# Differential attention's norms at other units, an 8 KB factor spread, split tables and a re-ordered first and last stretch in a two-layer decoder trunk

## The reference, cut to what matters

```python
for l in range(2):
    h = rmsnorm(x, norm_mix[l])
    u, sq, sk, sv, dq, dk, dv, gate_logits = split(h @ w_in[l])
    y_ssm = gelu(s5_ssm(u, lam_re, lam_im, log_dt, b, c, d))   # 32 groups, 64 complex states each
    glu_a, glu_b = split(y_ssm @ w_glu[l]);  y_ssm = glu_a * sigmoid(glu_b)
    y_sb = stick_breaking_attention(sq, sk, sv)                # 8 heads of 64
    o = differential_attention(rope(dq), rope(dk), dv, lam)    # 4 heads, v of 128
    o = rmsnorm(o, diff_subln[l]) * (1 - lam_init)             # over each head's 128
    proj = einsum('bsnc,ncd->bsnd', [y_ssm, y_sb, o], w_branch[l])
    x = x + sum(sigmoid(gate_logits) * proj) @ w_out[l]
    x = x + cross_attention(rmsnorm(x, norm_cross[l]), rmsnorm(mem, norm_mem[l]))
    x = x + square(relu(rmsnorm(x, norm_mlp[l]) @ w_up[l])) @ w_down[l]
return rmsnorm(x, norm_final)
```

## Time and profile before

| | us |
|---|---|
| median of 3 runs | 1058.99 |
| lowest, highest run | 1057.1, 1062.11 |
| the profiled execution, its own time | 1057.28 |
| its span, first to last instruction | 1055.6 |
| TensorE busy in the span | 998.8 |
| VectorE busy | 765.9 |
| ScalarE busy | 557.3 |
| GpSimd busy | 45.8 |
| mean granted TensorE clock | 0.984 of full speed |

### The profile page before, as it was taken

How to read it: one execution, slowest core, us unless ns; L and a number is a source line. 1 busy time by engine, 2 the same in 40 slices (tenths; PEclk the granted TensorE clock), 3 DMA queues, 4 the chain that set the end, 5 groups by cost and what they waited for, 6 DMA issues and landing times. The chain is left out here.

```text
span 1055.6 us, 17635 instructions
## 1 busy us (share of the span) xinstructions
PE 998.8 (95%) x6784; PEld 884.1 (84%) x6784; DVE 765.9 (73%) x1186; ACT 557.3 (53%) x847; POOL 45.8 (4%) x100
## 2 busy tenths in 40 slices
PE   6989999979999999989999999998799999999996
PEld 6867899879897888878889779998798978888885
DVE  6979897758865866869865669786687658655664
ACT  7455435476655655535453663544647556444443
POOL 5003000000000004000000110000000000000000
PEclk9999999989999999999999999999899999999998
DMA  9894348435654665596646853564365445666661
GB/s 358 208 200 145 121 130 251 140 102 180 186 154 136 224 187 178 193 204 192 188 138 201 173 159 105 138 198 145 104 183 172 142 138 180 186 193 186 191 187 74
DMA packets 71827, 181.37 MB, mean 172 GB/s; under 512 B 27392, under 2 KB 29696, under 8 KB 71360
## 3 DMA queue, kind: packets, MB, share of 16 engines
q1 hardware_dynamic: 71600, 180.23, 58.2%
q10 hardware_dynamic: 144, 0.00, 0.0%
HBM read 176.67 MB, written 3.54 MB: 171 GB/s over the span
## 5 line engine op out<-in xcount | busy, mean ns | idle before, releaser
L1262 DVE TENSOR_TENSOR s_w_lo<-s_raw,s_w_hi 128x1024 fp32r<-128x1024 f32 x312 | 374.3, 1227 | 93.6 <-ACT s_w_hi L905 90.4
L905 ACT ACTIVATE s_w_hi<-s_raw 128x1024 fp32r<-128x1024 f32 x312 | 321.1, 1054 | 189.4 <-PE p_T L1845 76.3
L1843 PE MATMUL p_T<-s_hT,s_w_hi 128*128 128x256 f32 x576 | 165.8, 288 | 0.1
L1844 PE MATMUL p_T<-s_hT,s_w_hi 128*128 128x256 f32 x576 | 162.9, 283 | 0.0
L1845 PE MATMUL p_T<-s_hT,s_w_lo 128*128 128x256 f32 x576 | 162.8, 283 | 0.0
L1843 PE MATMUL p_A<-s_w_hi,s_bT_hi 128*128 128x512 f32 x320 | 125.3, 391 | 5.3 <-DVE s_w_lo L1262 2.8
L1845 PE MATMUL p_A<-s_w_hi,s_bT_lo 128*128 128x512 f32 x320 | 124.7, 390 | 0.0
L1844 PE MATMUL p_A<-s_w_lo,s_bT_hi 128*128 128x512 f32 x320 | 124.6, 390 | 0.0
L1843 PEld LDWEIGHTS p_T<-s_hT,s_w_hi 128*128 128x128 f32 x576 | 110.3, 191 | 4.0 <-issue 2.7
L1844 PEld LDWEIGHTS p_T<-s_hT,s_w_hi 128*128 128x128 f32 x576 | 110.4, 192 | 0.1
L1845 PEld LDWEIGHTS p_T<-s_hT,s_w_lo 128*128 128x128 f32 x576 | 110.3, 192 | 0.0
(11 more groups left out here) (265 smaller groups left out, 1872.9 us busy)
## 6 DMA issues: line engine op xcount, KB each, us to landing
s_raw<-in_weights SPq DMA_DIRECT2D x312, 512.0 KB, 3.6
s_bt<-in_ssm_bt SPq DMA_DIRECT2D x2, 1024.0 KB, 11.9
s_gates<-f_turn SPq DMA_DIRECT2D x16, 128.0 KB, 8.8
s_x<-in_x SPq DMA_DIRECT2D x1, 1024.0 KB, 9.2
s_dv<-in_ssm_bc SPq DMA_DIRECT2D x2, 512.0 KB, 8.0
u_turn<-s_st_y SPq DMA_DIRECT2D x4, 256.0 KB, 5.2
s_uB<-u_turn SPq DMA_DIRECT2D x16, 64.0 KB, 4.8
s_bt<-in_mem SPq DMA_DIRECT2D x1, 1024.0 KB, 6.9
```

The lines of the kernel that those rows point to most:

```text
L905: return nc.scalar.activation(o, i, f, **kw)
L1262: return V.tensor_tensor(o, i0, i1, op)
L1843: mm(o, lhi, rhi, start=first, stop=False, **kw)
L1844: mm(o, lhi, rlo, start=False, stop=False, **kw)
```

## The change

It has six parts.

1. `da_n` of the first tile goes from unit 24 to 22; `da_o` 0, `da_c` 1 and `da_n` 1 go from unit 26 to 25. `da_o` 1 stays at 27.
2. The table of factors is stored by four transfers of 256 byte runs instead of two of 512 byte runs, in an order that lets each of the eight spreading loads read 8 KB in one run for each of its 16 partitions.
3. Layer 0's phase tables: steps 0 and 1 at unit 0 (a new stage `p_ph0`, which runs in the `stage` part), 2 and 3 at unit 6, 4 at 7, the products of step 5 at 8 and its sums at 9. Steps 0 to 3 use part of `gates` as scratch. `p_bt` 0, 1, 2 go from units 9, 10, 11 to 10, 11, 12.
4. `e16` is made on GpSimd at the start.
5. Start: ScalarE issues `x_t` part 0, `col` and `positions`; SyncE goes from chunk 0 on to `x_t` part 1. ScalarE rounds chunk 0 before it waits for `col`. VectorE's `rope_angles` (nine small operations) comes behind its work on `x_t`. `bt` is loaded behind chunk 12.
6. End: x times the last gain is done in two halves of 512 columns, the first ahead of the last unit's residual; ScalarE makes the bias after the first half's squares and takes Ln of each tile as its square is there; VectorE makes one factor `RC` and scales columns 0 to 639, ScalarE scales 640 to 1023; a store waits for both.

```diff
+END = 640
-        for k in range(TAB_STEPS):
-            after(u["ph"][max(0, k - 3)], "p_ph", tgt, k)
+        for at, k, part in u["ph"]:
+            after(at, "p_ph", tgt, k, part)
-        pre(0, dict(ct=-1, f=(2, 3), cv=(3, 4), b0=5, ph=(7, 7, 8), bt=(9, 10, 11)))
+        pre(0, dict(ct=-1, f=(2, 3), cv=(3, 4), b0=5, 
+                    ph=((6, 2, 2), (6, 3, 2), (7, 4, 2), (8, 5, 0), (9, 5, 1)), bt=(10, 11, 12)))
+        after(0, "p_ph0")
...
-    after(24, "da_n", 0)
-    after(26, "da_o", 0)
-    after(26, "da_c", 1)
-    after(26, "da_n", 1)
+    after(22, "da_n", 0)
+    after(25, "da_o", 0)
+    after(25, "da_c", 1)
+    after(25, "da_n", 1)
     after(27, "da_o", 1)
...
-                    dst = f_turn[t].rearrange("(n r i) s -> r n i s", r=2, n=BL)
                     for r in range(2):
-                        load(dst[r], fT[PC * r:PC * r + PC, :], f_out)
+                        for h in range(2):
+                            load(f_turn[t, :, h, STILES * r:STILES * r + STILES, :], fT[PC * r:PC * r + PC, PC * h:PC * h + PC],
+                                 f_out)
...
-                            load(bF[p:p + GC].rearrange("p r (i s) -> p (r i) s", s=STATES),
-                                 src[h, j].unsqueeze(0).broadcast_to([GC, 2 * STILES, STATES]), f_in)
+                            load(gates[p:p + GC, 0:8, :].rearrange("p k n -> p (k n)"),
+                                 f_turn[t, j, h].rearrange("k s -> (k s)").partition_broadcast(GC), f_in)
...
                     if l == 0 and c == 0:
-                        load_params(0)
-                        load_x_t(0)
                         load_x_t(1)
...
-                    if l == 0 and c == 6:
+                    if l == 0 and c == 12:
                         load_b(0)
...
+            act.dma_start(x_t[:, X_PARTS[0], :], a["x_t"][:, X_PARTS[0], :]).then_inc(xt_landed[0].sem, 16)
+            act.dma_start(col[:, :], a["col"][0]).then_inc(prm_landed.sem, 16)
             act.dma_start(stat[:, 62:64].bitcast(I32), a["positions"]).then_inc(pos_landed, 16)
...
-                    if which == "mix":
+                    if which == "mix" and l:
                         act.wait_ge(*st.at(prm_landed, l + 1))
...
                     if which == "mix" and l == 0:
-                        rope_angles()
                         for i, part in enumerate(X_PARTS):
...
+                        rope_angles()
                         return
...
-                        for q in range(4):
-                            n = 2 * GC * q
-                            tt(e16[n:n + 2 * GC, :], ident[n:n + 2 * GC, n:n + GC], ident[n:n + 2 * GC, n + GC:n + 2 * GC],
-                               ALU.add).then_inc(*st.mid())
-                        dve.wait_ge(*st.mine())
+                        dve.wait_ge(consts_made, 20)
...
-                def p_ph(t, k):
+                def p_ph(t, k, part=2):
...
+                    scratch = st_y[:, :, :].rearrange("p r n -> p (r n)")
+                    if t == 0 and k < 4:
+                        scratch = gates[:, 12, :]
+                    elif t == 0:
+                        dve.wait_ge(*st.at(u_out, 2))
+                    q = scratch[:, 0:2 * STILES * n].rearrange("p (r i n) -> p r i n", r=2, n=n)
+                    if part != 1:
+                        tt(o, e, c[0]).then_inc(*st.mid())
+                        tt(q, e, c[1]).then_inc(*st.mid())
+                        dve.wait_ge(*st.mine())
+                    if part:
+                        tt(o[:, 0], o[:, 0], q[:, 1], ALU.subtract).then_inc(*st.mid())
...
+                    elif kind == "p_ph0":
+                        for k in range(2):
+                            p_ph(0, k)
+                            dve.wait_ge(*st.mine())
...
+                    if l + 1 == DEPTH and u + 1 == NU:
+                        dve.wait_ge(nf_landed, 16)
+                        dve.wait_ge(*st.mine())
+                        gained(0)
...
+            gained(1)
             dve.wait_ge(end_act, 8)
...
+            V.tensor_tensor(RC, R0, TT, ALU.mult).then_inc(*est.mid())
+            dve.wait_ge(*est.mine())
             for t in range(NT):
-                V.tensor_scalar(xn[:, t, :], xn[:, t, :], R0[:, t:t + 1], TT[:, t:t + 1], ALU.mult, ALU.mult)\
-                 .then_inc(*est.mid())
+                V.tensor_scalar(xn[:, t, 0:END], xn[:, t, 0:END], RC[:, t:t + 1], None, ALU.mult).then_inc(*est.mid())
```

More of the change, by code:

```diff
@@ L513, in hybrid_trunk @@
         bt_landed = counted("bt_landed", DEPTH, step=16)
-        f_out, f_in = counted("f_out", 2 * DEPTH, step=16), counted("f_in", 2 * BL * DEPTH, step=16)
+        f_out, f_in = counted("f_out", 4 * DEPTH, step=16), counted("f_in", 2 * BL * DEPTH, step=16)
         k_out, k_in = signal("k_out", 4, step=16), signal("k_in", 2 * BL, step=16)
@@ L768, in _ @@
             for t in range(NT):
-                sp.wait_ge(end_dve, 7 + t)
+                sp.wait_ge(end_dve, 10 + t)
+                sp.wait_ge(end_scaled, 1 + t)
                 sp.dma_start(out[0].rearrange("(t p) d -> p t d", p=P)[:, t, :], xn[:, t, :]).then_inc(stored, 16)
@@ L804, in tt @@
                 return nc.gpsimd.tensor_tensor(o, i0, i1, op)
+            for q in range(4):
+                n = 2 * GC * q
+                tt(e16[n:n + 2 * GC, :], ident[n:n + 2 * GC, n:n + GC], ident[n:n + 2 * GC, n + GC:n + 2 * GC], ALU.add)\
+                    .then_inc(*cst.mid())
+            pool.wait_ge(*cst.mine())
             def tables(st, t):
@@ L956, in norm @@
                                 prep_chunk(i // 2)
+                            act.wait_ge(*st.at(prm_landed, 1))
                             act.wait_ge(*st.at(xt_landed[i], 1))
@@ L1202, in _ @@
                     if half:
-                        act.wait_ge(end_act, 1 + t)
+                        act.wait_ge(end_act, 3)
                     c = slice(512 * half, 512 * half + 512)
@@ L1206, in _ @@
                         .then_inc(end_act, 1)
-            act.wait_ge(end_act, 4)
-            fn(SS0V, SS, ACT.Identity, scale=1.0 / D, bias=eps[:, 0:1]).then_inc(end_act, 1)
-            act.wait_ge(end_act, 5)
-            for t in range(NT):
-                fn(R0[:, t:t + 1], SS1[:, t:t + 1], ACT.Ln, scale=1.0 / D, bias=SS0V[:, t:t + 1]).then_inc(end_act, 1)
+                    if half:
+                        act.wait_ge(end_act, 4 + 2 * t)
+                        fn(R0[:, t:t + 1], SS1[:, t:t + 1], ACT.Ln, scale=1.0 / D, bias=SS0V[:, t:t + 1]).then_inc(end_act, 1)
+                if half == 0:
+                    act.wait_ge(end_act, 2)
+                    fn(SS0V, SS, ACT.Identity, scale=1.0 / D, bias=eps[:, 0:1]).then_inc(end_act, 1)
             act.wait_ge(end_act, 7)
             fn(R0, R0, ACT.Exp, scale=-0.5).then_inc(end_act, 1)
+            act.wait_ge(end_dve, 9)
+            for t in range(NT):
+                fn(xn[:, t, END:], xn[:, t, END:], ACT.Identity, scale=RC[:, t:t + 1]).then_inc(end_scaled, 1)
         @block.vector
@@ L1255, in _, with gained @@
             dve.wait_ge(*pst.mine())
+            est = Steps(end_dve)
+            def gained(half):
+                c = slice(512 * half, 512 * half + 512)
+                for t in range(NT):
+                    V.tensor_tensor(xn[:, t, c], x[:, t, c], uB_flat[:, c], ALU.mult).then_inc(*est.mid())
             for l in range(DEPTH):
@@ L1799, in _ @@
                 dve.wait_ge(*st.mine())
-            est = Steps(end_dve)
-            dve.wait_ge(nf_landed, 16)
-            for t in range(NT):
-                V.tensor_tensor(xn[:, t, :], x[:, t, :], uB[:, :, :].rearrange("p i n -> p (i n)"), ALU.mult)\
-                 .then_inc(*est.mid())
+            gained(1)
             dve.wait_ge(end_act, 8)
```

23 lines of the change are left out of this document (8 added, 15 removed).

## The result

The changed kernel takes 1027.67 us, the median of four runs (1026.68 to 1028.59); the kernel before took 1058.72 us in the four runs now at hand (1057.1 to 1062.11). The ratio is 0.9702, with a 95% interval of 0.9676 to 0.9729: 31 us faster. The forecast was 1029.0 us, from a sum of 29.95 us. The profiled execution after took 1026.68 us, with a span of 1025.0 us; against the 1057.28 and 1055.6 us before, that is 30.6 us by either.

The account below looks back on a forecast made before the run. TensorE, busy nearly throughout, bounds the kernel; gains come only from its waits, low clock and ends. Norms 22.2, spread 2.75, tables 4.4 less 0.3, start -0.3, end 1.2 sum to 29.95 us: 1059.0 to 1029.0 us, range 1024 to 1034.

Parts of the forecast that it names:

- e16: Work moved from VectorE to GpSimd at the start: takes 0.76 us off VectorE's lateness, costs nothing on GpSimd, idle until 11.5.
- 214.5: Norms: the time in us when VectorE ends the second norm, before TensorE is through unit 27 at about 218.
- the drain of a table load: Norms: counting the skill's 2.66 us for load and drain would make the gain about 0.8 us less a layer.
- the limit of 12: Second spread: a transfer of anything up to 12 us was held early enough for TensorE; some 5 us were taken.
- the bound of 3: Second spread, first layer's MLP: upper bound in us of the gain, forecast at 2.75 with lower bound 0.
- the wait and its low clock: Layer 0, ahead of `sb_u` 1: 2.75 us of wait and 1.65 us of low clock go, a gain of 4.4.
- the bound, not 0.3: Start and tables up to `mm_k`: a loss of 0.3 us, bounded by a gain of 1 and a loss of 1.5.
- A: Rival: half of the second norm's wait stays, with its low clock, 12.6 us worse, 1041.6 us; chance 0.12.
- B: Rival: the tables don't pay, the mask is late again, 4.4 us gone and 1 more lost, 1034.4 us; chance 0.12.
- C: Rival: the new waits (0.85 and 0.6 twice) don't appear and the start gains 1 us, 1024.8 us; chance 0.10.
- D: Rival: the second spread still delays its chunk, 2.75 us worse, 1031.8 us; counted within the forecast's 0.63.
- E: Rival: one transfer engine carries each spreading load, eight take 43 us and stop TensorE, 1075 us; chance 0.02.

Follow-up runs that it names:

- third group: The group of runs in which the unaltered changed kernel was run again, 1027.42 us, beside the kernel before, 1055.9 us.
- norms_back: Changed kernel with `da_n` 0 back at unit 24 and `da_o` 0, `da_c` 1, `da_n` 1 back at unit 26: 1048.8 us.
- spread_back: Changed kernel with the factors stored and spread as before (two stores of 512 byte runs, eight loads of 256 byte runs): 1031.4 us.
- phases_at_6: Changed kernel with steps 0 and 1 of layer 0's phase table at unit 6 beside steps 2 and 3, none at unit 0: 1025.75 us.
- tables_back: Changed kernel with layer 0's tables as before (steps 0 to 4 at unit 7) and `e16` on VectorE again: 1030.12 us.

## Why the forecast was right, and where its steps were not

The parts, undone one by one, give 21.4 (norms), 4.0 (spread), 2.7 (tables), -0.9 (start) and 0.4 (end), 27.6 us together, by the medians. By the ratios, which take each group's own runs of the kernel before, the same five are 22.4, 4.6, 3.6, 0.2 and 1.4, 32.2 together. The whole difference in the third group is 28.5 us, in the result's own runs 31.0. The forecast's parts were 22.2, 2.75, 3.8 for tables and start together (4.4 less 0.3 and 0.3; 1.8 when undone), and 1.2. The store of the factors in four pieces and the later `bt` were not undone by themselves.

**Norms: right, with a cause missing.** Waits of 7.41 and 2.56 us gone, 0.83 ahead of `da_t` 7 (0.85 forecast), 0.51 ahead of unit 29 (0.6 forecast), the second norm done at 212.8 us (214.5 forecast, TensorE there at 215.90), and 11.30 and 11.32 us a layer against 11.1. The text priced the order alone; 2.64 us of the wait were table loads, and its 214.5 us fit only an answer as short as the first norm's (0.68 us), which the move did bring, for a reason that the text does not give. The low clock behind the long wait was put at 2.6 us; the traces of before and after, subtracted, have 2.7 in layer 0 and 2.6 in layer 1, `norms_back` 1.5 and 1.4. On the drain of a table load: in the kernel after the sigmoid again starts 1.30 us behind the load's start (211.21 and 212.51), so the row was the right one to use, and the figure of the Trainium skill ("ScalarE: Activation LUTs", What ACT_TABLE_LOAD costs), 2.66 us, is not seen here.

**Spread: right sign, wrong quantity.** Some 5 us were taken for the transfer, under the limit of 12. The chunk came 13.3 us behind the first issue, and TensorE did not wait, so the limit was too low as well. It is not far off: with the start undone 0.63 us of wait stood at that place. The gain of 3.16 us is just over the bound of 3; 2.76 us of it are the two waits (1.46 and 1.30) that are gone. When undone, the place cost 3.9 us, since the clock fell behind the wait there, which in the kernel before it did not (1.00). Layer 0's own spread was put at nothing, and beside the old tables no wait hung on it; beside the new ones it is worth 0.85 us (`spread_back`).

**Tables: the wait and its low clock are right (4.51 against 4.4).** The wait ahead of unit 3 was put at 1.4 us and is 0.74; the wait at `mm_k` went from 1.60 to 0.81. By `phases_at_6`, steps 0 and 1 at unit 0 cost 1.2 us at `mm_k`. `ssm_in` 0 lost 0.58 (0.3 forecast, bounds 0 to 1.5). Not seen beforehand: 0.41 us ahead of `da_t` 0. In layer 0 VectorE's work on `ssm_in` 3 ends 2.02 us earlier than before, TensorE would have been there 2.42 us earlier, and its bank is held until then.

**Start: the step that failed** is "ScalarE rounds chunk 0 when it lands, about 0.7 us earlier, and TensorE starts at about 7.75". The chunk was rounded 0.7 us later, at 5.78 instead of 5.08 us, and TensorE started at 9.14, because ScalarE's queue had the first part of x in flight beside it. Even with that part back on SyncE's queue the chunk was used at 4.92, only 0.16 us before the 5.08 of before: the 0.7 us that were put down to the wait for `col` were hardly there to win. Nor did the start matter: at `mm_k` the old and the new one are level. The loss at `mm_k` was 1.5 us, the bound, not 0.3, and it is only partly explained. Steps 0 and 1 at unit 0 make 1.2 us of it, `e16` on GpSimd gives back some 1.0 (`tables_back` and `phases_at_6` differ in little else up to there), and about 1.3 us more are in neither the tables nor the start as they were undone; they stay open. The rule in the Trainium skill ("DMA: Bandwidth & Descriptors", Issuing engines are not separate DMA queues), that transfers of all queues interleave on the same engines, fits the rows of chunk 0. Its other half, that the issuing time is saved, is seen as well: SyncE issued the third part of x at 2.19 instead of 3.15 us. Nothing of it reached TensorE.

**End: right by the trace of the engines.** The last scale was ready 1.17 us earlier behind the last product; 0.89 us arrived at the end, since the stores took 4.0 instead of 3.7 us from there. From the last product to the end it is 8.24 us, not the "under 8" that the forecast named as a sign of being right.

**The sum** came within 0.65 us of the profiled difference. That is partly luck: at `mm_k` and `da_t` 0 the changed kernel was 1.6 us worse off than forecast, and 1.58 us of clock in layer 1's first products, which the kernel after loses as well in another execution, made up for it.

**Rivals.** A fell: no part of the long wait stayed. B fell: the mask was on time. C fell: the new waits came, and the start did not gain. D and E fell: TensorE did not wait for the chunk behind the second spread, and eight loads of 16 partitions together with that chunk took 13.3 us, not the 43 that one engine would need.

## What to carry to other kernels

Ask of every long answer between engines what it is made of: here a third of the longest wait was two table loads that one call, made while the engine was idle, hides with nothing moved. Where one engine has hardly a pause over a long stretch, an earlier start of another engine changes nothing behind it; its own work, added or taken away there, moves the rest. A transfer given to a second queue can hold back the first one's most urgent transfer. And one trace of a kernel is one execution: before a difference at a low clock is put down to a change, see whether other traces have it.

## What the runs showed of the hardware

The low clock behind one and the same wait is not certain. Behind the 2.56 us ahead of unit 26 the kernel before lost 0.4 us in each layer. With the norms back and the table loaded early, the same wait was followed by 1.9 us of loss in layer 0 and by 0.4 in layer 1. Behind 1.32 us of wait at the start of layer 1 the clock fell in four of fourteen traces. It fits with this that a kernel with long waits scatters more: over the groups the kernel before ran from 1053.1 to 1063.7 us, the changed one from 1026.7 to 1028.6. No run isolates it.

In TensorE's first microseconds the column of the granted clock does not tell the pace. It reads 1.00 from 11.2 to 14.2 us, where each product of 256 columns starts 0.213 us behind the one before, the pace of 1.2 GHz; later products of the same form come each 0.12 us. How long this first stretch lasts differs too, from 2.9 to 6.1 us behind the first product over the fourteen traces.

A broadcast of 128 KB from memory to 16 partitions occupies the issuing queue for 0.42 us (median) with runs of 8 KB. With runs of 256 bytes the median is 0.75 to 0.89 us and the longest 4.8 us: the first four of eight took 0.50 us each and the last four 1.5, while the transfer engines were full and moved 90 GB/s. A weight chunk issued behind them then took 1.40 us to issue instead of 0.42.
